# The gate projections of a two-layer diffusion block's merge, as jobs in the attention stages

## The reference, cut to what matters

```
h_l = modulate(rms_norm(x, norm1), mod_l[0], mod_l[1])
z = jnp.concatenate([h_c, h_l], axis=1) @ w_in
...
oa_l = from_heads(neighbourhood_attention(qa_l, ka_l, va_l, ka_c, va_c, na_rpb))
ob_l = from_heads(block_attention(qb_l, ...))          # latent attention, "mla"
oc_l = gla_output(oc_l_raw, zl[11], gla_o_norm)        # gated linear attention, "gla"
y_l = gated_merge(oa_l, ob_l, oc_l, zl[12], zl[13], zl[14], w_br_a, w_br_b, w_br_c, w_out)
...
def gated_merge(o_a, o_b, o_c, m_a, m_b, m_c, w_br_a, w_br_b, w_br_c, w_out):
    y = (jax.nn.sigmoid(m_a) * (o_a @ w_br_a) + jax.nn.sigmoid(m_b) * (o_b @ w_br_b)
         + jax.nn.sigmoid(m_c) * (o_c @ w_br_c))
    return y @ w_out
```

## Time and profile before

| what | value |
|---|---|
| median of 3 runs | 3082.44 us (3052.95 to 3086.1) |
| the profiled execution | 3058.77 us |
| its span, first to last instruction | 3056.5 us |
| PE busy | 2717.5 us (89%) |
| DVE, ACT, POOL busy | 1012.9, 686.0, 33.4 us |
| mean granted TensorE clock | 0.922 |

### The profile page before, as it was taken

How to read it: one execution, slowest core, us unless ns; L and a number is a source line. 1 busy time by engine, 2 the same in 40 slices (tenths; PEclk the granted TensorE clock), 3 DMA queues, 4 the chain that set the end, 5 groups by cost and what they waited for, 6 DMA issues and landing times.

```text
span 3056.5 us, 42212 instructions
## 1 busy us (share of the span) xinstructions
PE 2717.5 (89%) x17806; PEld 1793.1 (59%) x17806; DVE 1012.9 (33%) x2091; ACT 686.0 (22%) x1306; POOL 33.4 (1%) x59
## 2 busy tenths in 40 slices
PE   5999998899988599999999689897799958999996
PEld 3888765688876535453444578775578743333332
DVE  4535344543233512312222544423343431111112
ACT  2511133322121211111111352123332221101101
POOL 1000000000000000000000000000000000000000
PEclk9999887989998599999999899956899979999998
DMA  5111552612222079786968111220023229999996
GB/s 187 49 42 37 167 197 83 194 28 69 70 97 84 28 294 351 293 350 260 382 258 349 58 58 45 56 55 1 1 62 104 83 110 361 390 399 379 410 384 240
DMA packets 233951, 539.78 MB, mean 177 GB/s; under 512 B 9734, under 2 KB 102128, under 8 KB 233776
## 3 DMA queue, kind: packets, MB, share of 16 engines
q1 hardware_dynamic: 231008, 531.34, 47.0%
q0 software_dynamic: 2768, 5.87, 0.9%
HBM read 532.91 MB, written 4.26 MB: 176 GB/s over the span
## 4 chain that ended last, share of the span: by engine, by line
PE 81%; DVE 8%; DMA 5%; ACT 4%; issue 2%; SPq 0%; DVEq 0%; POOL 0%; ACTq 0%
PE ps L1152 15%; PE ps L827 12%; PE ps L1219 11%; PE ps L1349 5%; PE ps L1061 4%; DMA arena<-in_moe_w_up 3%; PE ps L1170 3%; PE ps L1368 3%; PE ps L1391 2%; PE ps L1035 2%; PE ps L1412 2%; PE ps L1242 2%; PE ps L1246 2%; PE ps L1044 2%; PE ps L796 2%
## 5 line engine op out<-in xcount | busy, mean ns | idle before, releaser
L1219 PE MATMUL ps<-arena 128*32 128x512 f32 x2304 | 342.8, 604 | 5.8 <-issue 4.8
L1220 PE MATMUL ps<-arena 128*32 128x512 f32 x768 | 342.4, 604 | 0.0
L1349 PE MATMUL ps<-arena 128*64 128x512 f32 x1024 | 236.9, 609 | 34.6 <-DMA arena<-in_moe_w_up 31.3
L827 PE MATMUL ps<-m_lo,h_hi 128*128 128x256 f32 (+1 forms) x1248 | 243.5, 296 | 5.5 <-DVE m_lo L1882 3.9
L1219 PEld LDWEIGHTS ps<-arena 128*32 128x32 f32 x2304 | 94.1, 112 | 227.8 <-issue 225.2
L1152 PE MATMUL ps<-h_hi,m_hi 128*128 128x512 f32 (+1 forms) x576 | 205.6, 357 | 6.9 <-DVE m_lo L2387 6.9
L827 PEld LDWEIGHTS ps<-m_lo,h_hi 128*128 128x128 f32 x1248 | 201.5, 200 | 17.4 <-issue 12.8
L1152 PE MATMUL ps<-h_lo,m_hi 128*128 128x512 f32 (+1 forms) x576 | 205.2, 356 | 0.0
L1152 PE MATMUL ps<-h_hi,m_lo 128*128 128x512 f32 (+1 forms) x576 | 204.9, 356 | 0.0
L1349 PEld LDWEIGHTS ps<-arena 128*64 128x64 f32 x1024 | 74.5, 139 | 184.5 <-issue 180.8
L827 PE MATMUL ps<-m_lo,h_lo 128*128 128x256 f32 (+1 forms) x624 | 180.3, 289 | 0.0
(11 more groups left out here) (358 smaller groups left out, 4548.0 us busy)
## 6 DMA issues: line engine op xcount, KB each, us to landing
arena<-in_moe_w_gate SPq DMA_DIRECT2D x128, 1024.0 KB, 7.9
arena<-in_moe_w_up SPq DMA_DIRECT2D x128, 1024.0 KB, 8.8
arena<-in_moe_w_down SPq DMA_DIRECT2D x128, 1024.0 KB, 8.3
ring<-in_ada_w SPq DMA_DIRECT2D x20, 2048.0 KB, 7.9
ring<-in_w_in SPq DMA_DIRECT2D x54, 512.0 KB, 5.1
ring<-in_w_in SPq DMA_DIRECT2D x18, 1024.0 KB, 5.1
ring<-in_w_out SPq DMA_DIRECT2D x4, 2048.0 KB, 8.6
arena<-in_ada_w SPq DMA_DIRECT2D x3, 2048.0 KB, 21.0
```

Of the source, the lines that this page charges most:

```text
L827: last = mm(to, stationary, moving, start=at == 0 and k == 0, stop=at == 2 and k == KD - 1)
L1219: mm(ps[r][32 * b:32 * b + 32, :], c_xg[:, k, j, 32 * b:32 * b + 32], w, start=k == 0, stop=k == KD - 1)
L1220: last = mm(ps[r][96:128, :], c_xg[:, k, j, 32 * r:32 * r + 32], up[:, kk, 512:1024], start=k == 0, stop=k == KD - 1)
L1349: last = mm(bank[64 * c:64 * c + 64, :], p_xg[:, k, j, :], p_raw[(i + c) % PAIR_SLOTS][:, kk, 512 * half:512 * half + 512], start=k == 0, ...
```

## The change

The gate projections leave the merge. They become jobs (`mix_jobs`): 48 in layer 0 (8 channel blocks x 3 branches x 2 segments) and 24 in layer 1, each of 24 matmuls. A table, `MIX_AT`, places half jobs of 12 matmuls in the iterations of both attentions and in the tile loop of `latent_heads`. In layer 0 both places of an iteration are filled in all 24 na units, in the 6 latent tiles and in 18 mla units. In layer 1 an iteration takes one half job, and every third takes two: 22 half jobs in the 16 na iterations, 8 in four latent tiles, 18 in 14 mla iterations. The weights come through the chunk slots (12 more chunks of 256 columns a layer). DVE copies a finished job from PSUM (`mix_taken`), POOL stores it to DRAM (`mix_spill`), and the merge loads three gates of a block at a time into one of three slots (`MIX_SLOTS`); ACT applies the sigmoid in place. The branch weights get four slots (`W_SLOTS`).

Other things move with it. An iteration of an attention is now `scores(u)`, modulation products, half job, `values(u-2)`, modulation sums, the four latent transposes of u-1, half job, the two context transposes of u-1. The values' output lies in the bank of the context transposes, so these wait for `o_ok`. The sums of units lie in four columns, so the exponentials of u wait for `normalise` of u-4. The `dkv` jobs of layer 1 go ahead of the attention, as in layer 0. The modulation's weights are loaded in halves. In the merge `y` and `w_out` are split step by step (`OUT_STEPS`).

```diff
-M_AT = (0, KD + 2, 2 * KD + 4)
 MT = 4 * KD
+W_SLOTS, MIX_SLOTS = 4, 3
...
+MIX = len(CHUNKS)
+CHUNKS += tuple([(O_M + b * D + 256 * i, 256)] for i in range(KD // 2) for b in range(3))
...
-        UNITS_AHEAD = {"na": 2, "mla": 0}
+        UNITS_AHEAD = 2
...
+        def mix_jobs(l):
+
+            return [(MIX + 3 * i + b, P * c, seg, 2 * i + c, b) for i in range(KD // 2) for b in range(3) for c in range(2) for seg in segments(l)]
+
+
+        MIX_AT = ([("na", u, place) for u in range(24) for place in (0, 1)] + [("lat", t, place) for t in range(NT) for place in (0, 1)]
+                  + [("mla", u, place) for u in range(18) for place in (0, 1)],
+                  [("na", u, place) for u in range(16) for place in ((0, 1) if u % 3 == 0 else (0,))]
+                  + [("lat", t, place) for t in range(1, NT - 1) for place in (0, 1)]
+                  + [("mla", u, place) for u in range(14) for place in ((0, 1) if u % 3 == 0 and u < 12 else (0,))])
...
+        def mix_bank(l, stage, i):
+            if stage == "lat":
+                return ps[2 + i % 2] if l else ps[2]
+            return ps[6 + i % 2] if l else ps[6]
...
+        OUT_STEPS = [[], [("y", 0)], [("y", 1)], [("y", 2), ("w", 4)], [("y", 3), ("w", 5)], [("y", 4), ("w", 6)], [("y", 5), ("w", 7)],
+                     [("y", 6), ("w", 0), ("w", 1), ("w", 2), ("w", 3), ("y", 7)]]
+        OUT_ORDER = [item for step in OUT_STEPS for item in step]
+        OUT_K = (4, 5, 6, 0, 1, 2, 3, 7)
...
+                for stage in ("na", "lat", "mla"):
+                    for u in range(NT if stage == "lat" else UNITS[l]):
+                        if l == 0 and stage != "lat" and u < 2 * ADA[stage]:
+                            ada_load(stage, 2 * ada_first(stage) + u)
+                        i = mix_ended(l, stage, u)
+                        if i is not None and i + 1 < len(mix_jobs(l)) and mix_jobs(l)[i][0] != mix_jobs(l)[i + 1][0]:
+                            if mix_jobs(l)[i][0] + 2 < len(CHUNKS):
+                                chunk_load(l, mix_jobs(l)[i][0] + 2)
+                sp.wait_ge(mix_up, before("mix_up", l + 1))
...
+            def merge_load(l, j):
+                if j >= W_SLOTS:
+                    sp.wait_ge(m_ok, before("m_ok", l) + 3 * NSEG[l] * (j - W_SLOTS + 1))
+                for b in range(3):
+                    sp.dma_start(raw_weights(j)[:, w_tiles(b), :],
+                                 a[("w_br_a", "w_br_b", "w_br_c")[b]][l][:, j * P:(j + 1) * P].rearrange("(k p) n -> p k n", p=P)
+                                 ).then_inc(w_in[j % W_SLOTS], 16)
+                if j == MIX_SLOTS:
+                    out_load(l, 0)
+                if j >= MIX_SLOTS:
+                    sp.wait_ge(m_ok, before("m_ok", l) + 3 * NSEG[l] * (j - MIX_SLOTS + 1))
+                for done in mix_stored:
+                    sp.wait_ge(done, before("mix_stored", l) + 8 * sum(job[3] <= j | 1 for job in mix_jobs(l)))
+                cols = slice(q_tiles(l)[0] * P, TOK)
+                sp.dma_start(mix_gates(j)[:, :, cols], mix_spill[l][j, :, :, cols]).then_inc(mix_in[j % MIX_SLOTS], 16)
...
+                for i, (_, _, seg, j, b) in enumerate(mix_jobs(l)):
+                    pool.wait_ge(mix_copied, before("mix_copied", l) + i + 1)
+                    pool.dma_start(mix_spill[l][j, :, b, seg], mix_out[i % 2][:, 0:seg.stop - seg.start]).then_inc(mix_stored[i % 2], 16)
...
+            def mix_steps(l, stage, u, place):
+
+                at = mix_half(l, stage, u, place)
+                if at is None:
+                    return
+                i, half = at
+                m, c0, seg, _, _ = mix_jobs(l)[i]
+                _, w_hi, w_lo = chunk_parts(m)
+                to, cols = mix_bank(l, stage, i)[:, 0:seg.stop - seg.start], slice(c0, c0 + P)
+                for k in range(KD // 2 * half, KD // 2 * (half + 1)):
+                    if k == 0:
+                        split_there(l, NJ[l] + i)
+                        first = i == 0 or MIX_AT[l][2 * i][0] != MIX_AT[l][2 * i - 1][0]
+                        if i > (0 if l == 0 or first else 1):
+                            pe.wait_ge(mix_copied, before("mix_copied", l) + (i if l == 0 or first else i - 1))
+                    for n, (w, h) in enumerate(((w_hi, h_hi), (w_hi, h_lo), (w_lo, h_hi))):
+                        last = mm(to, w[:, k, cols], h[:, k, seg], start=n == 0 and k == 0, stop=n == 2 and k == KD - 1)
+                    if k == KD - 1:
+                        last.then_inc(mix_up, 1)
...
+                def turn_context(u):
                     if u:
                         pe.wait_ge(p_dve, before("p_dve", idx) + u)
+                        pe.wait_ge(o_ok, before("o_ok", idx) + u)
                     for t in range(CT):
                         last = tr(ps[5][:, tile(t)], prob[:, u % 2, tile(t)], ident)
                     last.then_inc(p_up, 1)
...
                     keys = range(NT if t >= CT else CT)
                     for kt in keys:
                         v = nav[:, kt, 64 * h:64 * h + 64] if i == 0 else mv[:, kt, h, :]
-                        last = mm(ps[6 + u % O_BANKS[l]][:, 0:64], probT[:, u % 2, kt, :], v, start=kt == 0, stop=kt == keys[-1])
+                        last = mm(ps[5][:, 256:320], probT[:, u % 2, kt, :], v, start=kt == 0, stop=kt == keys[-1])
                     last.then_inc(o_up, 1)
 
+                stage = ("na", "mla")[i]
                 for u in range(n + 2):
                     if u < n:
                         scores(u)
                     if l == 0:
-                        modulation_products(unit_events(("na", "mla")[i], u, "early"))
-                    if 1 <= u <= n:
-                        turn(u - 1)
-                    if l == 0:
-                        modulation_products(unit_events(("na", "mla")[i], u, "later"))
-                    if i == 0:
-                        project_between(l, u)
+                        modulation_products(unit_events(stage, u, "early"))
+                    mix_steps(l, stage, u, 0)
                     if u >= 2:
                         values(u - 2)
                     if l == 0:
-                        modulation_products(unit_events(("na", "mla")[i], u, "last"))
+                        modulation_products(unit_events(stage, u, "last"))
+                    if 1 <= u <= n:
+                        turn_latent(u - 1)
+                    mix_steps(l, stage, u, 1)
+                    if 1 <= u <= n:
+                        turn_context(u - 1)
...
+                    for place in (0, 1):
+                        mix_steps(l, "lat", t, place)
                     turn(t)
...
+                            for k in kts:
+                                if j == 0 and si == 0:
+                                    pe.wait_ge(part_lo, split_count(l, "o", k))
+                                hi, lo = high_weights(j)[:, k, :], low_weights(j)[:, k, :]
+                                for i, (w, x) in enumerate(((hi, oT_hi), (hi, oT_lo), (lo, oT_hi))):
+                                    last = mm(ps[2 * (q % 4) + 1][:, 0:size], w, x[:, k, seg], start=i == 0 and k == kts[0],
+                                              stop=i == 2 and k == kts[-1])
...
-                        act.wait_ge(o_ok, before("o_ok", idx) + u - 1)
-                    c = 32 + 8 * (u % 2)
+                    if u >= 4:
+                        act.wait_ge(o_ok, before("o_ok", idx) + u - 3)
+                    c = 32 + 8 * (u % 4)
...
+                            do(gates[:, b, seg], gates[:, b, seg], ACT.Sigmoid).then_inc(m_sig, 1)
...
+                    for kind, k in OUT_STEPS[j]:
+                        out_high(kind, k, 0)
...
+            def mix_taken(l, stage, u):
+
+                i = mix_ended(l, stage, u)
+                if i is None:
+                    return
+                _, _, seg, _, _ = mix_jobs(l)[i]
+                size = seg.stop - seg.start
+                dve.wait_ge(mix_up, before("mix_up", l) + i + 1)
+                if before("mix_up", l) + i >= 2:
+                    dve.wait_ge(mix_stored[i % 2], before("mix_stored", l) + 16 * (i // 2))
+                v.tensor_copy(mix_out[i % 2][:, 0:size], mix_bank(l, stage, i)[:, 0:size]).then_inc(mix_copied, 1)
+                if split_behind(l, NJ[l] + i) is not None:
+                    chunk_low(l, split_behind(l, NJ[l] + i))
...
+                            dve.wait_ge(m_up, before("m_up", l) + q + 1)
                             br = ps[2 * (q % 4) + 1][:, 0:size]
                             if b == 0:
-                                v.tensor_tensor(yT[:, j, seg], sig[q % 2][:, 0:size], br, ALU.mult).then_inc(m_ok, 1)
+                                v.tensor_tensor(yT[:, j, seg], gates[:, b, seg], br, ALU.mult).then_inc(m_ok, 1)
                             else:
-                                link(v.tensor_tensor(branch[:, 0:size], sig[q % 2][:, 0:size], br, ALU.mult))
```

(3 more changed lines are left out.)

300 lines of the change are left out of this document (135 added, 165 removed).

## The result

The changed kernel takes 2951.16 us (median of four runs, 2950.57 to 2953.12); before, run beside it, 3076.18 (3052.95 to 3086.1). The ratio is 0.9605, 95% interval 0.9548 to 0.9663: faster by about 4%. The forecast was 2980 with a range of 2940 to 3030. The profiled execution took 2951.56 us with a span of 2949.8, against 3058.77 and 3056.5 before, so 106.7 us went from span to span. The sum of the prediction has 84 there. PE runs 17806 matmuls in both.

What follows compares the result with a forecast made beforehand. PE was taken as the bound, busy most of the span but at 1.2 GHz in much of layer 1's na attention. Gains of 22.5 and 69.5, less 8, took 3058.8 to 2975; spread made it 2980 us, range 2940 to 3030.

Steps and rivals of the forecast that it cites:

- The rival in which the clock stays down: Layer 1's attentions stay at 1.2 GHz despite the half jobs, so the kernel is slower, 3168 us; chance 0.06.
- The merge that is left: Both layers' merges without gate projections: losses of 9 us in layer 0 and 7 in layer 1.
- DVE now decides: In the remaining merges DVE, not PE, sets the pace: 8.7 us a block in layer 0, 6.1 in layer 1.
- Collisions: Splits, copies and stores collide on DVE in 72 jobs, about 0.1 us each: 8 us taken off the gain.
- Layer 0, na: Layer 0's na attention: 200.5 us with 24 jobs, 90.5 more for 101 moved in, gain 10.
- Layer 0, mla: Layer 0's mla attention: 120 us becomes 181, 61 more for 75.6 moved, 4 off for clock; gain 10.
- Layer 1, na: Layer 1's na attention, largest term: 141 us instead of 124 for 60.5 moved, if clock holds 2.4 GHz; gain 43.
- The latent heads: Latent head tiles take jobs at less than full time: gain 5 us in each layer.
- the splits before the output projection: The splits ahead of the output projection go, ending a PE pause: 6.5 us gained in each layer.
- layer 1, mla: Layer 1's mla attention: 94 us becomes 121, 27 more for 49.5 moved; gain 22.
- From the profile to the median: Whole kernel: the median before lies 24 us above the profiled run; a quarter was added, taking 2975 to 2980 us.
- More than I count: Rival: warm attention ends and better merge overlap return the deductions and another 10 us, 2941 us; chance 0.14.

Runs made afterwards that it cites:

- The bunch: Changed kernel with all 24 gate jobs of layer 1 in one run ahead of its na attention, none in attentions and heads: 2997.05 us.
- the filler: Kernel before, plus 12 unused matmuls of 512 columns in each of units 7 to 15 of layer 1's na attention: ratio 0.9997.
- the kernel with the order alone: Kernel before with the new attention order, four sum columns and early dkv jobs, gate projections still in the merge: four runs, 3057.15 to 3118.5 us.
- the kernel with the late low part: Changed kernel with DVE's low part of a weight chunk set behind the context copy: 2949.79 us.
- jobs in the gaps: Changed kernel with 14 half jobs moved to na attention ends and before latent heads, mla half jobs spread, low part behind context copy: 2937.94 us.

## Why the prediction was right, and where its sizes were off

The mechanism was right, and so was the place of most of the gain. Layer 1's two attentions give 63 us of the 107, against 65 in the forecast. In the na attention they do it by the clock. The bunch shows that (45 us for those jobs' places alone), and the filler shows that such products raise it. In the mla attention about half of the 25 us is idle time filled, and the kernel with the order alone gets 21 of them without a job, which the prediction didn't see: it held the looser chain for what makes room, not for a gain by itself. The rival in which the clock stays down fell in every window of layer 1. The rule of the Trainium skill that I set beside that rival (TensorE: Matmul & The Clock Gate, the HAM clock gate) I had read as if a busy PE could not be helped by more work. The filler speaks against that reading: PE was busy in every microsecond at 0.50, and with 12 products of 512 columns an iteration the granted clock was 1.00. The same page of the Trainium skill says, under PE-mode transpose, that transposes don't count as busy in the way matmuls do. No run here shows whether that is the cause: transposes are a fifth of the slow iteration (2056.56 to 2057.90 us in the trace of before, 1.34 of 6.78), and none separates them from the thin scores and values.

The time itself was 29 us too high: the gain was 23 us larger than the 84 of the sum, and the 5 or 6 put on for the spread weren't needed. By the terms of the sum:

- **The merge that is left** (forecast loss 16, measured 6). The step "DVE now decides" failed. I added DVE's start-to-start intervals and estimates of 0.45 and 0.35 us for 256 columns to 8.7 and 6.1 us a block; DVE's busy time is 64.33 / 8 = 8.0 and 45.62 / 8 = 5.7, and PE's, 69.17 / 8 = 8.6 and 47.03 / 8 = 5.9, is the longer. The two paces differ by little, so this step cost the sum only some 2 us. Most of the 10 us is the start: the 6 to 8.5 us for the mixers' splits are 2.8 and 2.3 us of wait, and they fall before the first product, outside the merges' 69.9 and 47.2. The loss of 9 in layer 0 is also a slip: 70 + 8.5 against the 273 - 202 = 71 to be had is 7.5.
- **Collisions** (8 taken off, little measured). No DVE wait for a store shows; a store of 256 KB by POOL lands in 2.4 us, as against the 5.8 that I took from gathers, and PE waits 3.8 and 2.4 us in all for late context copies in layer 1's two attentions, more than 0.1 us a job. But these waits are hardly a loss in the sum: the kernel with the late low part, where they are 1.6 and 1.2 us, is 1.4 us faster at the median, within the spread.
- **Layer 0, na** (10, measured 17). The sum after was right to a microsecond (200.5, measured 201.5), the base was not: the 110 us of the window end at 452, and the last values of the two last iterations come at 460.9. I counted 5 us for these iterations after and left them out before.
- **Layer 0, mla** (10, measured 13): the stage was to take 181 us and took 182.1. The 4 us that I took off for a falling clock at its end weren't lost; the clock is 1.00 in 754 to 784 us, the iterations without a job, and falls only behind them.
- **Layer 1, na** (43, measured 38). A half job is 2.90 us, not 2.75, and the single iteration 7.02, not 6.63; ten of them make 4 us. The double ones were 8.98 in the forecast and are 9.15.
- **The latent heads** (10 together, measured 9), **the splits before the output projection** (13, measured 14) and **layer 1, mla** (22, measured 25) were about right. The pause before the projection is gone as said.
- **From the profile to the median** (5 added). The changed kernel has no such distance. What spread before was for the most part the attentions' clock, and the low clock is gone from most of them. So the gain between medians (125 us) is larger than between the profiles (107), whose one of before was a good run.

Two of three signs that I named showed: iterations of 7.02 and 9.15 us at clock near 1.00, and no pause. Of the third, the merges ran in 69.9 and 47.2 us, just below both bands, and DVE was not full (64.33 of 70 us). The result lies nearer to the rival *More than I count* (2941) than to the forecast, and for two of its three reasons: the losses in the merge and the collisions were too high.

## What to carry to other kernels

Look for stages in which PE is busy and its granted clock low: in this kernel products of 512 columns there cost less than their time, down to nothing, and work taken from a dense stage was worth 46 us more spread through such a stage than put ahead of it. Put some into the pauses between such stages as well (13 us here). Look first whether a looser order fills the stage by itself, as in the mla attention, before counting on the jobs for it. When a stage is compared before and after, both must be cut at the same instructions; and once a stage is emptied, look at which loads it now has to take in half the time, since slots that were enough for blocks of 22 us (175.9 / 8) are not for blocks of 6.

## What the chip showed that I had not expected

- A PE busy for 56 of 56 us ran at 1.2 GHz all that time, with jobs of 24 products of 160 columns in it, and an iteration with 12 more products of 512 columns was faster than without (6.38 against 6.78 us).
- 131 us of dense products just ahead of the attention didn't keep its clock: 0.50 in 2100 to 2180 us.
- The same order of instructions is worth 1 us an iteration in the mla attention at 2.4 GHz (3.85 against 4.83 us) and nothing in the na attention at 1.2 (7.12 against 6.78).
- The spread of before from run to run (3052 to 3093 us in 42 runs) went with its mean granted clock (0.923 down to 0.902). Four runs of the changed kernel lie within 2.6 us; with jobs in the gaps six runs still spread by 13 us.
